# A decoder step on one core: the logits' Tanh, the first expert's high parts and the first rows' turning, each moved to an earlier stage

## The reference

```python
def route(x2d, router_w, router_bias):
    scores = jax.nn.sigmoid(jnp.dot(x2d, router_w, preferred_element_type=jnp.float32))
    sel = scores + router_bias.astype(jnp.float32)
    grp = sel.reshape(-1, N_EXPERT_GROUPS, EXPERTS_PER_GROUP)
    grp_score = jnp.sum(lax.top_k(grp, TOP_K)[0], axis=-1)
    g_idx = jnp.argmax(grp_score, axis=-1)
    in_grp = (jnp.arange(N_EXPERTS) // EXPERTS_PER_GROUP)[None, :] == g_idx[:, None]
    _, e_idx = lax.top_k(jnp.where(in_grp, sel, -jnp.inf), TOP_K)
    w = jnp.take_along_axis(scores, e_idx, axis=-1)
    w = w / jnp.sum(w, axis=-1, keepdims=True)
    return jnp.sum(jax.nn.one_hot(e_idx, N_EXPERTS, dtype=jnp.float32) * w[..., None], axis=1)
...
    for e in range(N_EXPERTS):
        h = jax.nn.silu(x2 @ w_gate[e]) * (x2 @ w_up[e])
        out = out + gates[:, e:e + 1] * (h @ w_down[e]).astype(jnp.float32)
```

## Time and profile before

| | |
|---|---|
| median of 3 runs | 1177.9 us (1174.29 to 1179.55) |
| the profiled execution, own time | 1176.98 us |
| its span (first to last instruction) | 1175.2 us |
| TensorE busy, share of the span | 1036.3 us, 88% |
| VectorE, ScalarE, GpSimd | 59%, 45%, 20% |

### The profile page before, as it was taken

The page is one execution under the profiler, slowest core; times in us unless marked ns, Lnnn a source line. Parts: engine busy times, 40 slices in busy tenths (PEclk is TensorE's granted clock), DMA queues, the critical chain, the costliest instruction groups (busy, mean ns, idle before and its releaser), DMA issues. The chain is left out here.

```text
span 1175.2 us, 17873 instructions
## 1 busy us (share of the span) xinstructions
PE 1036.3 (88%) x5490; PEld 857.7 (73%) x5491; DVE 692.5 (59%) x1392; ACT 528.8 (45%) x892; POOL 234.9 (20%) x558
## 2 busy tenths in 40 slices
PE   6998999899599999999992399999999999999920
PEld 5886879899366787688872378888888888888820
DVE  4556466341399932755546754466657678775537
ACT  4231332332478852622211244445546577665434
POOL 0713544720230000000000102122222222122110
PEclk9998999999699999999996599999999999999965
DMA  7130231201870051743320556687669899988455
GB/s 247 46 107 19 64 112 53 67 7 25 299 221 1 1 176 64 246 174 130 125 95 18 195 218 204 245 284 252 219 199 332 284 312 399 392 276 278 128 144 195
DMA packets 51105, 201.34 MB, mean 171 GB/s; under 512 B 8962, under 2 KB 15490, under 8 KB 44898
## 3 DMA queue, kind: packets, MB, share of 16 engines
q1 hardware_dynamic: 40530, 138.43, 33.1%
q0 software_dynamic: 7488, 27.27, 9.9%
q10 hardware_dynamic: 3024, 34.87, 7.7%
HBM read 163.80 MB, written 36.73 MB: 171 GB/s over the span
## 5 line engine op out<-in xcount | busy, mean ns | idle before, releaser
L2106 DVE TENSOR_TENSOR wlo<-raw,whi 128x1024 fp32r<-128x1024 f32 x192 | 221.6, 1218 | 42.1 <-ACT whi L2008 41.9
L2008 ACT ACTIVATE whi<-raw 128x1024 fp32r<-128x1024 f32 x192 | 186.9, 1048 | 67.1 <-issue 32.6
L1949 PE MATMUL psG<-whi,exs 128*128 128x512 f32 x200 | 81.8, 409 | 7.8 <-DVE exs L2111 7.8
L1949 PE MATMUL psY<-whi,ehs 128*128 128x512 f32 x200 | 81.1, 406 | 4.1 <-DVE wlo L2106 4.1
L1951 PE MATMUL psG<-whi,exs 128*128 128x512 f32 x200 | 79.5, 397 | 0.0
L1950 PE MATMUL psG<-wlo,exs 128*128 128x512 f32 x200 | 79.3, 397 | 0.0
L1914 POOL DMA_INDIRECT acc<-eyb,idxs x25 | 41.3, 1652 | 188.7 <-ACT eyb L2026 188.7
L1950 PE MATMUL psY<-wlo,ehs 128*128 128x512 f32 x200 | 79.0, 395 | 0.0
L1951 PE MATMUL psY<-whi,ehs 128*128 128x512 f32 x200 | 78.9, 395 | 0.0
L1951 PE MATMUL psU<-whi,exs 128*128 128x512 f32 x200 | 78.1, 390 | 0.0
L1949 PE MATMUL psU<-whi,exs 128*128 128x512 f32 x200 | 77.8, 389 | 0.0
(11 more groups left out here) (401 smaller groups left out, 2353.9 us busy)
## 6 DMA issues: line engine op xcount, KB each, us to landing
raw<-in_moe_w_gate SPq DMA_DIRECT2D x16, 2048.0 KB, 9.5
raw<-in_moe_w_up SPq DMA_DIRECT2D x16, 2048.0 KB, 9.7
raw<-in_moe_w_down ACTq DMA_DIRECT2D x16, 2048.0 KB, 8.6
w_raw<-in_w_in SPq DMA_DIRECT2D x27, 256.0 KB, 3.5
stg<-in_x_prompt SPq DMA_DIRECT2D x8, 512.0 KB, 4.2
kc<-in_cache_k SPq DMA_DIRECT2D x16, 256.0 KB, 3.0
vc<-in_cache_v SPq DMA_DIRECT2D x16, 256.0 KB, 3.0
mr<-in_w_out SPq DMA_DIRECT2D x8, 512.0 KB, 3.2
```

The lines of the kernel that those rows point to most:

```text
L1949: pe.matmul(out, hi, w_hi, start=(k == 0), stop=False)
L2008: nc.scalar.activation(whi[:, at], s.raw[:, at], ACT.Copy).then_inc(hi_made[i], 1)
L2106: nc.vector.tensor_tensor(wlo[:, at], s.raw[:, at], whi[:, at].bitcast(F32), ALU.subtract) \
```

## The change

Four things change. The logits are no longer copied and then put through Tanh in the router: in the mixing stage the first seven blocks are copied and put through one Tanh after the last block's root, and the last two are kept by a Tanh directly. The high parts of the first expert's gate and up weights are made by ScalarE in the router's stage; there also TensorE turns the first slot's rows, and ScalarE copies their high part. `whi`, the high part's tile of the first rows (`exs00`) and `psX` are therefore held from the router's stage on. The experts' stage starts without them: ScalarE loads the down weights, passes over the unlikely case (in which the high parts must be made anew, from the other expert's weights) and only then raises `hi_made`; VectorE takes the rows' low part first. In the router's stage the fills of `keep` and `pad_row` move behind the gates, and the tables' instructions are put in another order, some ahead of the wait for `placed`, with one pass over `past` fewer (`far` adds a large number to the end of unused experts, so that they need no product with `ne`).

```diff
@@ mix, ScalarE
-                    nc.scalar.activation(s.lgt[0:r, b, :], bk[6 + b % 2][0:r, 0:E], ACT.Copy).then_inc(l_kept, 1)
+                    func, scale = (ACT.Copy, 1.0) if b < QB - 1 else (ACT.Tanh, 0.5)
+                    nc.scalar.activation(s.lgt[0:r, b, :], bk[6 + b % 2][0:r, 0:E], func, scale=scale).then_inc(l_kept, 1)
...
+                    if b == QB:
+                        act.wait_ge(l_kept, QB - 1)
+                        nc.scalar.activation(s.lgt[:, 0:QB - 1, :], s.lgt[:, 0:QB - 1, :], ACT.Tanh, scale=0.5)
                     if b >= 1:
                         keep_logits(b - 1)
@@ route, ScalarE
-                nc.scalar.activation(sc[:, :, :], s.lgt[:, :, :], ACT.Tanh, scale=0.5).then_inc(tanhed, 1)
+                for i in range(2):
+                    for n in range(4):
+                        at = quarter(i, n)
+                        nc.scalar.activation(s.whi[:, at], s.raw[:, at], ACT.Copy)
+                act.wait_ge(s.x_turned, 1)
+                nc.scalar.activation(s.x_hi[:, :], s.psX[:, :], ACT.Copy).then_inc(s.x_kept, 1)
@@ route, TensorE, after the slot products
+                pe.wait_ge(s.gathered[0], 16)
+                xv = s.xg[0][:, :].rearrange("t (p k) -> t k p", k=KD)
+                for k in range(KD):
+                    last = pe.transpose(s.psX[:, k * P:(k + 1) * P], xv[:, k, :], s.ident[:, :])
+                last.then_inc(s.x_turned, 1)
@@ route, VectorE
-                nc.vector.memset(keep[:, :, :], 1.0)
                 nc.vector.memset(edge[:, 0, 0, :], 2.0)
...
-                ch(nc.vector.memset(keep[:, :, 0:1], 0.0))
-                ts(pad_row[:, :], tok[:, 0:1], float(N), None, ALU.add)
-                dve.wait_ge(tanhed, 1)
-                ch(ts(A(sc), A(sc), 0.5, 0.5, ALU.mult, ALU.add))
+                ch(ts(A(sc), s.lgt[:, :, :], 0.5, 0.5, ALU.mult, ALU.add))
...
                 tt(A(gate), A(gate), wide(ws[:, :], E), ALU.mult)
+                ch(nc.vector.memset(keep[:, :, :], 1.0))
+                ch(nc.vector.memset(keep[:, :, 0:1], 0.0))
+                ts(pad_row[:, :], tok[:, 0:1], float(N), None, ALU.add)
                 dve.wait_ge(counted, 1)
...
                 ch(ts(ne[:, :], nb[0:1, :], 0.0, None, ALU.is_gt))
+                ts(far[:, :], ne[:, :], -FAR, FAR, ALU.mult, ALU.add)
+                nc.vector.tensor_reduce(top[:, :], ne[:, :], AX.X, ALU.add)
+                ch(nc.vector.tensor_tensor_scan(w0[:, 0:E], ones[0:1, 0:E], ne[:, :], 0.0, ALU.mult, ALU.add))
+                tt(far[:, :], far[:, :], end[0:1, :], ALU.add)
+                ch(ts(w0[:, 0:E], w0[:, 0:E], ne[:, 0:1], None, ALU.subtract))
+                ch(tt(A(past), wide(count[0:1, 0:NSB + 1], E), mid(far[:, :], NSB + 1), ALU.is_ge))
+
                 dve.wait_ge(placed, 1)
...
-                ch(tt(A(past), wide(count[0:1, 0:NSB + 1], E), mid(end[0:1, :], NSB + 1), ALU.is_ge))
-                ch(tt(A(past), A(past), mid(ne[:, :], NSB + 1), ALU.mult))
-                ch(nc.vector.tensor_reduce(eb[:, :], A(past), AX.X, ALU.add))
...
@@ experts, TensorE
-                turn_x(0, 0, 1)
-
@@ experts, ScalarE
                 for i in range(3):
                     act.sem_inc(hi_made[i], 4)
-                high(0, 0)
-                keep_x(0, 0)
                 load_down(0)
                 with act.If(entry(act, 0, 0, 1, E) > 1):
+                    for i in range(2):
+                        act.wait_ge(w_in[i], 32)
+                        for c in range(4):
+                            at = quarter(i, c)
+                            nc.scalar.activation(whi[:, at], s.raw[:, at], ACT.Copy).then_inc(again, 1)
+                    act.wait_ge(again, 8)
                     act.wait_ge(w_in[2], 16)
                     load_down(1)
-                high(0, 1)
+                for i in range(2):
+                    act.sem_inc(hi_made[i], 4)
@@ experts, VectorE
+                low_x(0, 0)
                 low(0, 0)
-                low_x(0, 0)
                 low(0, 1)
```

More of the change, by code:

```diff
@@ L1580, with quarter @@
 WIDE = (NSB + 2) // 2 * 2
+FAR = 4096.0
+def quarter(i, c):
+    a, n = PIECES[i][0], (PIECES[i][1] - PIECES[i][0]) // 4
+    return slice(a + n * c, a + n * (c + 1))
 def route(nc, io, s):
@@ L1601, in route @@
         place, blk = sb("place", [P, 2, NBLK]), sb("blk", [P, 2, NBLK])
-        past = sb("past", [1, NSB + 1, E])
+        past, among = sb("past", [1, NSB + 1, E]), sb("among", [1, E, E])
+        far, es = sb("far", [1, E]), sb("es", [1, E])
         ne, top = sb("ne", [1, E]), sb("top", [1, 1])
@@ L1614, in route @@
         held = c.enter_context(nc.psum_tensor("ps_held", [P, 3, WIDE], F32))
-        (seq, tanhed, ones_set, m_ready, counted, holds_ready, same_ready, placed, held_ready, idx_ready) = (
-            sem("ro_" + n) for n in "seq tanhed ones m_ready counted holds same placed held idx".split())
+        (seq, ones_set, m_ready, counted, holds_ready, same_ready, placed, held_ready, idx_ready) = (
+            sem("ro_" + n) for n in "seq ones m_ready counted holds same placed held idx".split())
         parts = [slice(a, a + 6) for a in range(0, 2 * NBLK, 6)]
@@ L1748, in _ @@
                 stt(s.held[:, 0:NSB + 1], held[:, 0, 0:NSB + 1], -1.0, padded[:, :], ALU.add, ALU.add).then_inc(held_ready, 1)
+                nc.vector.tensor_reduce(eb[:, :], A(past), AX.X, ALU.add)
+                ch(tt(among[:, :, :], wide(count[0:1, 0:E], E), mid(w0[:, 0:E], E), ALU.is_gt))
                 nc.vector.tensor_copy(s.slot_gate[:, :], held[:, 1, 0:NSB + 1])
[L1751 to L1762, removed]
-                ch(tt(A(past), wide(count[0:1, 0:NSB + 1], E), mid(end[0:1, :], NSB + 1), ALU.is_ge))
-                ch(tt(A(past), A(past), mid(ne[:, :], NSB + 1), ALU.mult))
-                ch(nc.vector.tensor_reduce(eb[:, :], A(past), AX.X, ALU.add))
+                ch(nc.vector.tensor_reduce(es[:, :], among[:, :, :], AX.X, ALU.add))
                 ch(ts(eb[:, :], eb[:, :], 1.0, top[:, :], ALU.add, ALU.min))
+                ts(w0[:, 0:1], top[:, :], 1.0, None, ALU.add)
+                ts(s.order[:, :], es[:, :], E - 1.0, None, ALU.min)
                 nc.vector.tensor_copy(s.wtab[:, 1, :], eb[:, :])
@@ L1771, in _ @@
                 ch(tt(new[:, 1:], eb[:, 1:], eb[:, 0:NSB], ALU.subtract))
+                tt(s.slot_gate[:, :], s.slot_gate[:, :], held[:, 2, 0:NSB + 1], ALU.add)
                 nc.vector.tensor_copy(s.wtab[:, 2, :], new[:, :])
+                ts(es[:, :], count[0:1, 0:E], ne[:, 0:1], w0[:, 0:1], ALU.add, ALU.min)
+                ch(ts(nb[:, 0:1], end[:, E - 1:E], 0.5, -0.25, ALU.mult, ALU.add))
+                ts(s.slot_gate[:, :], s.slot_gate[:, :], 1.0 / ALPHA, None, ALU.mult)
+                ts(s.split_by[:, :], es[:, :], 4.0, None, ALU.mult)
+                ch(ts(nb[:, 0:1], nb[:, 0:1], MAGIC, None, ALU.add))
                 ch(ts(w0[:, :], eb[:, :], top[:, :], None, ALU.is_lt))
                 tt(s.wtab[:, 3, :], new[:, :], w0[:, :], ALU.mult)
-                ch(ts(nb[:, 0:1], end[:, E - 1:E], 0.5, -0.25, ALU.mult, ALU.add))
-                ch(ts(nb[:, 0:1], nb[:, 0:1], MAGIC, None, ALU.add))
                 ch(ts(nb[:, 0:1], nb[:, 0:1], MAGIC, None, ALU.subtract))
@@ L1801, in experts @@
         sem = semaphores(nc, c)
-        whi, wlo = sb("whi", [P, WCOLS], F32R), sb("wlo", [P, WCOLS], F32R)
+        whi, wlo = s.whi, sb("wlo", [P, WCOLS], F32R)
         idxc, xg, gathered = s.idxc, s.xg, s.gathered
-        xs = [[sb(f"exs{j}{i}", [P, D], F32R) for i in range(2)] for j in range(2)]
+        xs = [[sb(f"exs{j}{i}", [P, D], F32R) if i + j else s.x_hi for i in range(2)] for j in range(2)]
         hs = [[sb(f"ehs{j}{i}", [P, FE], F32R) for i in range(2)] for j in range(2)]
@@ L1814, in experts @@
         psY = c.enter_context(nc.psum_tensor("psY", [P, D], F32))
-        psX = c.enter_context(nc.psum_tensor("psX", [P, D], F32))
+        psX = s.psX
         psH = c.enter_context(nc.psum_tensor("psH", [P, FE], F32))
-        (idx_kept, x_turned, x_kept, x_split, g_made, gu_made, tanhed, halfway, act_done, h_turned, h_kept, h_split,
-         y_made, y_kept) = (sem("ex_" + n) for n in "idx_kept x_turned x_kept x_split g_made gu_made tanhed halfway "
+        x_turned, x_kept = s.x_turned, s.x_kept
+        (idx_kept, x_split, g_made, gu_made, tanhed, halfway, act_done, h_turned, h_kept, h_split,
+         y_made, y_kept) = (sem("ex_" + n) for n in "idx_kept x_split g_made gu_made tanhed halfway "
                             "act_done h_turned h_kept h_split y_made y_kept".split())
@@ L1823, in experts @@
         w_in = [sem(f"ex_w{i}") for i in range(3)]
+        again = sem("ex_again")
         z = [s.raw[:, b * D:(b + 1) * D] for b in range(NBLK)]
@@ L1851, in from_block @@
             return type(b) is not int or b >= n
-        def quarter(i, c):
-            a, n = PIECES[i][0], (PIECES[i][1] - PIECES[i][0]) // 4
-            return slice(a + n * c, a + n * (c + 1))
```

(4 more changed lines are left out.)

## The result

The changed kernel takes 1182.0 us (median of 7 runs), the kernel before 1175.5 in 7 runs: a ratio (of the means) of 1.0047, 95% interval 1.0026 to 1.0069. It is slower, by about the 0.5% that can be told from no change; 1172.6 had been forecast, and 1177.5 as the upper end.

The account below looks back on a forecast made before the run. TensorE's products were taken to bound the experts' stage, so an earlier first product counts: 0.3 (router's stage end) + 4.5 (into the experts) = 4.8 us, forecast 1172.6 us, range 1168 to 1177.5.

Parts of the forecast that it names:

- The Tanh: Mixing stage: table load and Tanh, 1.6 us, fit a 3.9 us ScalarE gap; router's scores start 1.4 us earlier.
- `keep` and `pad_row`: Router's stage: fills behind the gates cost 0.3 us, leaving the copy of the counts 1.1 us earlier (bounds 1.0 and 1.4).
- Tables: Router's stage, VectorE: about 1.8 us of instructions go into 2.51 idle, 0.7 left; worth nothing alone, only a cover.
- Turning: Router's stage: first rows turned after a 4.4 us gather; stage ends with ScalarE, 0.3 us earlier, or 0.5 later at 5.3.
- Into the experts: Start of the experts' stage: ScalarE's first table read to first product takes 3.3 us in place of 7.85, gaining 4.5.
- The branch: ScalarE, experts' start: skipping the longer unlikely case adds nothing by the 54 ns row; by the skill's rule a fetch might.
- The clock's second fall: Rival, second block of experts: the half clock at 688.1 to 691.5 doesn't come, 1.6 us more, gain 6.4, 1170.6; chance 0.15.
- 200 groups of them: Expert stage: TensorE's `psG` products waited 7.8 us in all for the low part of the gathered rows.
- The rival "slower": Experts' first block: granted clock stays low, 0.2 us more per product; all 48 slow gives about 1181; chance 0.05.
- Whatever moves the first product forward therefore moves the end forward, if the weights keep up: Expert stage: the opening step, by which time gained before the first product at 670.84 is gained at the end.
- a stretch of TensorE without a wait, of the same length: Expert stage, after the first product: a sign that the prediction holds, TensorE's stretch unchanged in length.
- 423.49 of 423.50 us busy: Expert stage, 691.5 to 1115: TensorE at granted clock 1.00, read as nothing but its own products counting.

Follow-up runs that it names:

- the old order: Changed kernel with equal operand places, router's tables again in the old order behind the wait for the slot products: first product at 35.12 us, against 35.19.
- all three places moved: Kernel before, with `whi`, `exs00` and `psX` placed as in the changed kernel, no work moved: ratio 1.0067, blocks every 18.14 us.
- all + 32: Kernel before, with a 32-byte pad ahead of `whi`, shifting all operands of the experts' products together: blocks every 17.74 us.
- `whi` at 64: Kernel before, with 32-byte pads ahead of and behind `whi`, so it alone begins on a multiple of 64: blocks every 18.07 us.
- the mixing stage's pads: Changed kernel with the 480-byte pad, plus two pads bringing `w_out`'s parts to the place of the rows' parts: 1168.92 us, ratio 0.9923.
- equal places: Changed kernel with a 480-byte pad ahead of `whi`, all experts' operands at 288 past a multiple of 512: 1171.49 us, ratio 0.9955.
- the pad of 32: Changed kernel with a 32-byte pad ahead of `whi` at the far end: ratio 1.0034, blocks in turn every 18.24 and 18.04 us.

## Why the prediction was wrong

What it summed was right, and what it left out decided.

- *The Tanh* lies in the gap where it was put (623.46, with 3.08 us of idle time left behind it) and the scores are read at 0.19 us. Right.
- *`keep` and `pad_row`.* The copy of the counts is 0.96 us earlier, 1.1 were taken and 1.0 was the lower bound; taken out alone, the Tanh's move came to 0.9. So 1.1 was slightly too much.
- *Tables.* 1.01 us of the idle time is left where 0.7 was forecast; VectorE ends them 3.7 us earlier, as worked out, and that is worth nothing, as the old order showed.
- *Turning.* The stage ends 0.27 us earlier (0.3 forecast), by ScalarE's drain, as named. The first gather landed 4.4 us after its issue, as taken; had it taken 5.3, the prediction's own sum gives an end 0.4 later than before, not 0.5.
- *Into the experts.* 3.36 us against 3.3.
- *The branch* took 0.05 us, and the semaphore increments came 0.12 later: no fetch was seen. By the Trainium skill ("Runtime: NRT & Kernel Launch", Instruction fetch mechanics) a taken branch whose target lies outside the instruction window must wait for a fetch; this trace shows no such wait, and whether the target lay outside the window isn't shown.
- *The clock's second fall* did not come after the change, as that rival had it, and 1.6 us with it. But it does not hang on the change alone: of the ten kernels here that start the experts as before, five had it and five had not (those with all three places moved, `psX` or `whi` at the far end alone, all + 32, `whi` at 64); of the seven that start them early only the one with the mixing stage's pads had it. With one execution of each looked at, it isn't shown whether the early start makes it rarer.
- *Two readings.* "200 groups of them" was misread: x200 counts products. Of the 7.8 us of waits 6.08 lie ahead of the first product and 1.74 ahead of the second block's; the sum didn't use it. The rival "slower" priced all 48 products of the first block's gate and up weights as newly slow; nine were at the low clock already, so by its own price the time would be 3 us longer, not 4 to 5.

The step that failed is the first: "Whatever moves the first product forward therefore moves the end forward, if the weights keep up". It held only for products that take what they took; "a stretch of TensorE without a wait, of the same length" was forecast, and it came without a wait and 7.7 us longer (512.06 in place of 504.36 from the first product to the end). The row it rested on, 423.49 of 423.50 us busy, said that nothing but the products counts; so a change in the products, by 2%, is 8 us, and it was priced at nothing because no product was edited. What did it was part of the change: three tiles held over from an earlier stage, one of them the operand that TensorE streams. The prediction named the work that the change moves and did not ask what it does to the layout. None of its rivals had this in it; the rival "slower" put its price on the clock, and that was 1.00 from 672.9 on. That the time came out slower, to which 0.05 had been given, was so for a reason that the prediction did not have.

The cause is shown in both directions: the places alone, without the work, cost 0.67%; the work with equal places gains 0.45%. The forecast gain of 4.8 was there at the first product (4.79: 0.27 at the stage's end, 4.5 in the experts' start, as summed). What stays open is how the hardware comes to it. It isn't a cost of each single product by its own two operands: with `whi` alone at the far end, at 0, and all others at 32 the products of `wlo`, whose operands agree, are followed later too (0.231 from a product of `wlo` to the next, against 0.227 before), and the same difference of 32 bytes cost 0.38 us a block in one place and 0.28 in another.

## What to carry to other kernels

Where TensorE is busy without a gap, a change that moves a buffer is a change to its products: lay the distance of two equal products before and after side by side (here 0.228 and 0.233 us) before looking for waits, since here neither the waits, the busy time nor the clock showed it. Let the addresses of the streamed and the loaded operand leave the same rest when divided by 256; a pad of a few hundred bytes turned 0.5% of loss into 0.5% of gain, and two pads took 5 ns off each product of an older stage that nobody had touched. And work moved off a path is worth what ends next: the tables' 2.7 us lay behind ScalarE's copy and gave nothing, the Tanh's move gave its 0.9.

## What the runs showed of the hardware

- Products of 128x128 by 512 columns (fp32r) at a granted clock of 1.00 started 0.227 to 0.228 us apart in the mean of a kernel when the SBUF addresses of both operands had the same rest over 256 bytes, 0.232 to 0.233 when `whi` or the rows' parts differed by 32 (0.233 by 64, in the changed kernel with the pad of 32), 0.229 when `whi` differed by 128, and 0.228 by 256. Equal rests of 64 in place of 32 made a block 0.05 us shorter. Neither the region of SBUF nor the bank of PSUM made a difference.
- GpSimd's drain at a stage's end lasted until its gathers had landed: 7.03 us in the kernel before, 6.92 after, ending 0.1 us behind the landing of the second gather (issued at 657.84, 5.2 us to landing, drain over at 663.1). In all 17 traces it ended 0.12 us behind that landing.
- ScalarE's drain at that stage's end lasted as long as its last activation: 1.05 us for one of 1.02.
